# Router of a product-key expert layer: 136 of 256 candidate sums, and expert numbers by a sum and a smallest absolute value

## Chip, cores and metric

One core of a Trainium2 chip runs the whole kernel, in one launch. The metric is the device time of that launch in microseconds (us).

## What is computed

A two-layer diffusion backbone works on 512 latent tokens and 256 context tokens, each a row of 1024 values. In each layer three token mixers (differential attention, a two-way mLSTM, a short gated convolution) are merged, and then comes an expert layer with product keys. The change lies in the router of that expert layer. Cut to what matters, with N tokens, 8 heads and K = 16:

```python
q = (x @ wq).reshape(N, 8, 2, 128)
s = einsum('nhpd,hpkd->nhpk', q, keys)               # 2 x 128 scores for a token and head
top_s, top_i = lax.top_k(s, K)                       # the 16 best of each half, sorted
cand = top_s[:, :, 0, :, None] + top_s[:, :, 1, None, :]
best_s, best = lax.top_k(cand.reshape(N, 8, K * K), K)
i1 = take_along_axis(top_i[:, :, 0], best // K, -1)
i2 = take_along_axis(top_i[:, :, 1], best % K, -1)
expert = i1 * 128 + i2                               # 16 experts for a token and head
gate = softmax(best_s)
# then, for each token t and each of its 8 * 16 experts e:
# y[t] += gate * gelu(u_tab[e] . x[t]) * v_tab[e]
```

The tables `u_tab` and `v_tab` have 16384 rows of 1024 values in each layer. The context's output isn't needed in layer 1, so the experts run for ten tiles of 128 tokens: six in layer 0 and four in layer 1.

## The kernel before

**Tiles and stages.** Tokens lie on the 128 partitions, in tiles of 128. Two tiles are a pair: pair 0 is the context, pairs 1 and 2 are the latents. A stage is a generator in the program of each engine (`norm1`, `qkv`, `da`, `mlp`, `ml`, `mc`, `mln`, `merge`, `route`), for one layer and one or more pairs. `schedule()` (L117) writes the order of stages out by hand, in segments. At the end of nearly every stage stands a barrier across TensorE, VectorE and ScalarE (L1496 on VectorE), which SyncE waits for too.

**Expert groups between the steps.** The expert work of a routed tile is cut into 64 groups of two experts per token (`GS = 2`). A group is: two indirect transfers of GpSimd (L1131), each of which gathers one row of 8 KB for each of 128 tokens (1 MB) into a ring of 8 slots; two dot products on VectorE (L2055); gelu, weights and two small diagonal matrices on ScalarE (L1471 to L1478); eight TensorE products (L796) that add the rows up and free the two slots. `walk()` (L347) puts groups between the steps of stages: after step n of a stage come as many groups as the table `QUOTAS` says, and this table is computed when the kernel is built, from estimated step costs (`steps()`, L83) that the change doesn't touch. So each engine has one fixed order of work. ScalarE and TensorE treat a group one place later than VectorE (`LAG_ACT` and `LAG_PE`).

**The five routing stages.** `route` runs five times, each time for one pair, with 8 heads of 4 steps: layer 0 for pairs 0, 1 and 2, layer 1 for pairs 1 and 2. The quotas give them 0, 25, 48, 41 and 29 groups. In this text they are called route A to route E, in this order. In the fourth, the groups come in bursts: 8 after head 1, 7 after head 2, 5 and 6 later, and then one or two after each step. GpSimd may gather for head h of a tile only when VectorE has written that head's expert numbers (semaphore `routed`, L2028).

**What a head costs, by engine.** TensorE makes queries and scores (L758 and the chains of L436), ScalarE copies them out (L1413, L1420) and takes the exponentials (L1425). VectorE does the rest, in `route` (L1968), for both tiles of the pair:
- steps 1 and 2: `top16` (L1953) on each half of the scores. For each tile it takes the maximum of 8, finds their places, replaces them, takes 8 more and finds their places: five passes over 128 scores, ten for two tiles;
- step 3: the 64 places found become floats (L2005), the 16 x 16 sums are made for two tiles in one instruction of 512 elements (L2006), `top16` makes its ten passes over 256 sums each, and a shift (L2011) and a mask (L2012) split a place into its two coordinates;
- step 4: the coordinates become floats (L2015), and each is turned into a key number by comparing with 0 to 15 (L2018), multiplying (L2021) and adding up (L2024), each of these as two instructions of 512 elements; then times 128 plus the layer's base (L2026), and the sum (L2028). `gates` of the head before follows (L1989, L1991).

Between these passes stand `drain` instructions, so that each reads what the one before has written.

Of the kernel before, what the change touches and what calls it, by code (L numbers as in the profile page):

```python
# [8 lines left out]
D, SEQ, CTX, DEPTH, P = 1024, 512, 256, 2, 128  # L9
# [10 lines left out]
PH, NK, TOPK, PEER_N = 8, 128, 16, 16384  # L20
ADA_W = 384
BIG = 1e30
RS = 8
GS = 2
GROUPS = PH * TOPK // GS
# [175 lines left out]
def build(nc, io):  # L201
    fp32, u32 = mybir.dt.float32, mybir.dt.uint32
    ALU, ACT, AX = mybir.AluOpType, mybir.ActivationFunctionType, mybir.AxisListType
    es = ExitStack()
    with es:
        sbuf = es.enter_context(nc.sbuf_tensor("arena", [P, 53200], fp32))
# [5 lines left out]
        def sem(name):  # L212
            return es.enter_context(nc.semaphore(name))
# [3 lines left out]
        def s(name):  # L217
            if name not in S:
                S[name] = sem(name)
            return S[name]  # L220

        def view(base, shape, parts=P):
            n = int(np.prod(shape))
            ap = sbuf[0:parts, base:base + n]
            if len(shape) == 2:
                return ap.rearrange("p (a b) -> p a b", a=shape[0])
            if len(shape) == 3:
                return ap.rearrange("p (a b c) -> p a b c", a=shape[0], b=shape[1])
            return ap
# [6 lines left out]
        def keep(n):  # L236
            at[0] += n
            return at[0] - n
# [14 lines left out]
        LAM = view(keep(DEPTH), [DEPTH])  # L253
        SS, MS, RT = view(keep(24), [24]), view(keep(24), [24]), view(keep(24), [24])
        MX, NM, SUM, RC, RL, INV0 = (view(keep(2), [2]) for _ in range(6))
        IOTA = view(keep(TOPK), [TOPK])
        N1A = view(keep(DEPTH * 2 * KD), [DEPTH, 2, KD])
        N1B = view(keep(DEPTH * 2 * KD), [DEPTH, 2, KD])
        N1G = view(keep(DEPTH * KD), [DEPTH, KD])
# [16 lines left out]
        IDX = sbuf[:, keep(NT * P):at[0]].bitcast(u32).rearrange("p (a b) -> p a b", a=NT)  # L276
# [5 lines left out]
        DN = at[0]  # L282
        RING_AT = 53200 - RS * 2 * D
        RING = view(RING_AT, [RS, 2 * D])
        DENSE = RING_AT - DN
# [57 lines left out]
        w_in = [sem(f"w_in{i}") for i in range(WSLOTS)]  # L343
        gathered = [sem(f"gathered{i}") for i in range(RS)]
        ROT = range(2, 8)
# [460 lines left out]
        def _(sp):  # L806
# [13 lines left out]
            def const(dst, src):  # L820
                sp.dma_start(dst, src).then_inc(s("const_in"), 16)
                n_const[0] += 16
# [7 lines left out]
            const(CVCW.rearrange("p a b c -> p (a b c)"), io["cvcw"])  # L830
            const(GATEB, io["gate_b"])
            const(N1G.rearrange("p a b -> p (a b)"), io["n1g_cols"])
            const(IOTA, io["iota"].to_broadcast([P, TOPK]))
            assert n_const[0] == CONST_DMAS * 16

            def ada_rows_by_group(l, g):
# [2 lines left out]
            for q in range(AQ):  # L839
                if q >= 2:  # L840
                    sp.wait_ge(s("ada_mm"), q - 1)
                for g in range(4):
                    i = (q % 2) * 4 + g
# [264 lines left out]
        def _(pool):  # L1108
# [7 lines left out]
            pool.affine_select(out=MASK[:, 0, :], in_=MASK[:, 0, :], compare_op=ALU.is_ge, fill=BIG, base=0, pattern=[[1, P]], channel_multiplier=-1)  # L1116
            pool.affine_select(out=MASK[:, 1, :], in_=MASK[:, 1, :], compare_op=ALU.is_ge, fill=BIG, base=0, pattern=[[-1, P]], channel_multiplier=1)
            for half in range(2):
# [365 lines left out]
        def _(dve):  # L1484
            V_ = nc.vector
            TT, TSC, STT = V_.tensor_tensor, V_.tensor_scalar, V_.scalar_tensor_tensor
# [6 lines left out]
            def bc(ap, shape):  # L1493
                return ap.to_broadcast(shape)
# [458 lines left out]
            def top16(vals, idx, sco, work):  # L1953
                for v, i_, sc, w_ in zip(vals, idx, sco, work):
                    V_.max(v[:, 0:8], sc)  # L1955
                dve.drain()
                for v, i_, sc, w_ in zip(vals, idx, sco, work):
                    V_.max_index(i_[:, 0:8], v[:, 0:8], sc)  # L1958
                    V_.match_replace(w_, v[:, 0:8], sc, -3e38)  # L1959
                dve.drain()  # L1960
                for v, i_, sc, w_ in zip(vals, idx, sco, work):
                    V_.max(v[:, 8:16], w_)
                dve.drain()
                for v, i_, sc, w_ in zip(vals, idx, sco, work):
                    V_.max_index(i_[:, 8:16], v[:, 8:16], w_)  # L1965
                dve.drain()

            def route(kind, l, pairs):  # L1968
                (p,) = pairs
                t0 = 2 * p  # L1970
                area = buf(l, p, "RA", [8, PW])
                sco, scw = area[:, 4:6], area[:, 6:8]
                small = DN + PLACE[l, p]["RSM"]
                bs2, eb, nmx, ssum = view(small, [2, 2, TOPK]), view(small + 64, [2, 2, TOPK]), view(small + 128, [2, 2]), view(small + 132, [2, 2])
                small += 136
                tsh, tif = view(small, [2, 2, TOPK]), view(small + 64, [2, 2, TOPK])
                ixu = sbuf[:, small + 128:small + 192].bitcast(u32).rearrange("p (a b c) -> p a b c", a=2, b=2)
                bb = sbuf[:, small + 192:small + 288].bitcast(u32).rearrange("p (c a b) -> p c a b", c=3, a=2)
                bf, ie = view(small + 288, [2, 2, TOPK]), view(small + 352, [2, 2, TOPK])
                wide = DN + PLACE[l, p]["RW"]  # L1980
                cand, candw = (view(wide + 512 * i, [2, TOPK, TOPK]) for i in range(2))
                hot = (cand, candw)
                four = [P, 2, TOPK, TOPK]
                dve.wait_ge(s("h2_out"), nxt("h2_out", 32))
                dve.wait_ge(s("x1_out"), nxt("x1_out", 32))

                def gates(h):
                    dve.wait_ge(s("best_exp"), nxt("best_exp"))
                    V_.reciprocal(ssum[:, h % 2], ssum[:, h % 2])  # L1989
                    dve.drain()  # L1990
                    TT(GATE[:, t0:t0 + 2, h * TOPK:(h + 1) * TOPK], eb[:, h % 2], bc(ssum[:, h % 2].unsqueeze(2), [P, 2, TOPK]), ALU.mult)  # L1991
                    dve.drain().then_inc(s("gated"), 1)

                for h in range(PH):
                    bs_ = bs2[:, h % 2]
                    for pp in range(2):
                        n = 2 * h + pp
                        (b,), _, (f_,) = UNIT["s", l, p, n]
                        dve.wait_ge(bank_out[b], f_ + 1)
                        halves = [slice(i * P, (i + 1) * P) for i in range(2)]  # L2000
                        top16([tsh[:, pp, i, :] for i in range(2)], [ixu[:, pp, i, :] for i in range(2)],
                              [sco[:, pp, o] for o in halves], [scw[:, pp, o] for o in halves])
                        dve.drain().then_inc(s("top"), 1)
                        yield
                    V_.tensor_copy(tif, ixu)  # L2005
                    TT(cand, bc(tsh[:, 0].unsqueeze(3), four), bc(tsh[:, 1].unsqueeze(2), four), ALU.add)  # L2006
                    dve.drain()
                    flat = lambda a, i: a[:, i].rearrange("p a b -> p (a b)")
                    top16([bs_[:, i, :] for i in range(2)], [bb[:, 0, i, :] for i in range(2)], [flat(cand, i) for i in range(2)], [flat(candw, i) for i in range(2)])
                    TSC(nmx[:, h % 2].unsqueeze(2), bs_[:, :, 0:1], -1.0, None, ALU.mult)  # L2010
                    TSC(bb[:, 1], bb[:, 0], 4, None, ALU.logical_shift_right)  # L2011
                    TSC(bb[:, 2], bb[:, 0], 15, None, ALU.bitwise_and)  # L2012
                    dve.drain().then_inc(s("best"), 1)
                    yield
                    V_.tensor_copy(bf, bb[:, 1:3])  # L2015
                    dve.drain()
                    for i, o in enumerate(hot):
                        TT(o, bc(bf[:, i].unsqueeze(3), four), bc(IOTA.unsqueeze(1).unsqueeze(1), four), ALU.is_equal)  # L2018
                    dve.drain()
                    for i, o in enumerate(hot):  # L2020
                        TT(o, o, bc(tif[:, i].unsqueeze(2), four), ALU.mult)  # L2021
                    dve.drain()
                    for i, o in enumerate(hot):
                        V_.reduce_sum(ie[:, i], o, AX.X)  # L2024
                    dve.drain()
                    TSC(ie[:, 0], ie[:, 0], float(NK), float(l * PEER_N), ALU.mult, ALU.add)  # L2026
                    dve.drain()
                    TT(IDX[:, t0:t0 + 2, h * TOPK:(h + 1) * TOPK], ie[:, 0], ie[:, 1], ALU.add).then_inc(s("routed"), 1)  # L2028
                    if h:
                        gates(h - 1)  # L2030
                    if h == PH - 1:
                        gates(h)
                    yield
                barrier()
# [51 lines left out]
    return np.cos(ang).astype(np.float32), np.sin(ang).astype(np.float32)  # L2086


# [43 lines left out]
```

## Time and profile before

| | us |
|---|---|
| median of three runs | 5707.03 |
| lowest and highest of them | 5704.67, 5711.7 |
| span of the profiled execution | 5713.0 |

The profile page gives no other time for the profiled execution than its span, so the span stands for it: 6.0 us above the median of the runs and 1.3 us above the highest. TensorE is busy for 72% of the span, VectorE for 51%, ScalarE for 30% and GpSimd for 25%. No engine is busy all the time, because the stages have different limits. The chain that ended last is made of TensorE's chains of products (L436, 25% of the span), the gathers (18%), TensorE's products for the groups (L796, 9%) and VectorE's dot products (L2055, 6%), and then of many small shares, VectorE's top-16 lines among them. How to read such a profile here: the share of an engine over the whole span says little; the question is what binds in each of the five routing stages, and so most of the rows below are cut to those stretches.

### The profile page before, as it was taken

Reading aid. Unit: us, or ns where it says so; the run is one execution under the profiler, and the core shown is the slowest. Engines: PE = TensorE matmul, PEld = TensorE weight load, DVE = VectorE, ACT = ScalarE, POOL = GpSimd, SP = SyncE. Lnnn points to the kernel's source line nnn. Section 1 sums busy time; section 2 is a strip of 40 time slices with the busy share of each in tenths; the row PEclk is TensorE's granted clock in tenths of the full one; section 3 lists DMA queues with packets and bytes.
Section 4 is the critical chain, followed back from the end, with each engine's and each line's share of the span. In section 5 each row is a group of like instructions: output and inputs, shape, how many; then the busy total and the mean of one; then the engine's idle time right before and its main releaser. Section 6 shows DMA issues by size and latency. Waiting matters only on the chain.

```text
span 5713.0 us, 63933 instructions
## 1 busy us (share of the span) xinstructions
PE 4133.3 (72%) x22248; PEld 2503.9 (44%) x22248; DVE 2896.5 (51%) x6835; ACT 1716.0 (30%) x4747; POOL 1446.2 (25%) x1295
## 2 busy tenths in 40 slices
PE   3889668889896687658566677778566797645555
PEld 1678545566573354324222234667324564311111
DVE  1321757635447745874455443321685445954454
ACT  0200126333343343333322222200234253322222
POOL 0000012212222233333344341000231222345443
PEclk7879879979998898879788788759778898877777
DMA  6425448747798799999999995114896799899998
GB/s 256 160 107 173 158 167 295 269 170 295 288 370 326 287 409 395 390 364 383 371 416 411 396 421 221 48 41 162 316 370 236 282 401 372 307 359 421 403 421 353
DMA packets 259316, 1712.66 MB, mean 300 GB/s; under 512 B 37712, under 2 KB 39344, under 8 KB 71600
## 3 DMA queue, kind: packets, MB, share of 16 engines
q0 software_dynamic: 184320, 1342.26, 59.0%
q1 hardware_dynamic: 74672, 366.31, 17.4%
q8 instruction: 176, 2.88, 0.2%
q14 instruction: 148, 1.21, 0.1%
HBM read 1690.43 MB, written 17.92 MB: 299 GB/s over the span
## 4 chain that ended last, share of the span: by engine, by line
PE 41%; DMA 22%; DVE 17%; ACT 6%; issue 4%; DVEq 4%; POOL 3%; ACTq 2%; PEld 1%; SPq 1%; PEldq 0%; POOLq 0%
PE psum L436 25%; DMA arena<-in_uv,arena 18%; PE psum L796 9%; DVE arena L2055 6%; POOL arena L1131 3%; DMA arena<-in_w_ada 1%; DVE arena L1965 1%; DVE arena L1958 1%; PEld psum L436 1%; PE psum L396 1%; DVE arena L1959 1%; PE psum L617 1%; PE psum L618 1%; ACT arena L1226 1%; DMA arena<-in_w_mix 1%
## 5 line engine op out<-in xcount | busy, mean ns | idle before, releaser
L1131 POOL DMA_INDIRECT arena<-in_uv,arena x1280 | 1442.3, 1127 | 4231.1 <-PE psum L796 2795.7
L796 PE MATMUL psum<-arena 64*64 64x512 f32 x10240 | 1559.2, 738 | 934.0 <-ACTq L1478 854.4
L2055 DVE CUSTOM_DVE_ANT_0 arena<-arena 128x1024 f32<-128x1024 f32 x1280 | 1547.2, 1226 | 1121.4 <-DMA arena<-in_uv,arena 1055.0
L436 PE MATMUL psum<-arena 128*128 128x256 f32 (+2 forms) x8480 | 1958.0, 389 | 111.1 <-DVEq L1497 80.9
L436 PEld LDWEIGHTS psum<-arena 128*128 128x128 f32 (+1 forms) x8480 | 1618.6, 195 | 563.6 <-issue 192.0
L796 PEld LDWEIGHTS psum<-arena 64*64 64x64 f32 x10240 | 388.1, 156 | 1864.1 <-ACTq L1478 1176.1
L1471 ACT ACTIVATE arena<-arena 128x2 f32<-128x2 f32 x640 | 130.8, 204 | 1620.4 <-DVEq L2057 1605.0
L1477 ACT ACTIVATE arena<-arena 128x64 f32<-128x64 f32 x1280 | 375.9, 340 | 46.1 <-issue 2.1
L396 PE MATMUL psum<-arena 128*128 128x128 f32 (+1 forms) x680 | 128.1, 343 | 298.4 <-DVE arena L1556 102.5
L1474 ACT ACTIVATE arena<-arena 128x1 f32<-128x1 f32 x1280 | 307.9, 287 | 45.1 <-issue 0.7
L1917 DVE TENSOR_TENSOR arena<-arena,psum 128x256 f32<-128x256 f32 x120 | 50.6, 421 | 460.3 <-ACT arena L1381 458.6
L396 PEld LDWEIGHTS psum<-arena 128*128 128x128 f32 (+1 forms) x680 | 96.6, 177 | 353.2 <-issue 154.3
L1471 ACT ACT_TABLE_LOAD x158 | 202.7, 1283 | 31.9 <-DVEq L2057 28.2
L1381 ACT ACTIVATE arena<-psum 128x256 f32<-128x256 f32 x120 | 46.0, 384 | 394.8 <-PE psum L436 394.6
L2055 DVE DVE_READ_ACCUMULATOR2_ANT arena<- 128x1 f32 x1280 | 105.8, 83 | 0.0
L1381 ACT ACT_TABLE_LOAD x69 | 88.5, 1283 | 51.5 <-PE psum L436 42.5
L1955 DVE MAX8 arena<-arena 128x8 f32<-128x128 f32 (+1 forms) x240 | 69.6, 332 | 67.8 <-ACT arena L1420 55.4
L1612 DVE TENSOR_REDUCE arena<-psum 128x2 f32<-128x1536 f32 (+1 forms) x40 | 61.8, 1545 | 73.9 <-PE psum L522 73.4
L1205 ACT ACTIVATE arena<-psum 128x256 f32<-128x256 f32 x68 | 26.1, 384 | 226.0 <-PE psum L436 225.9
L537 PE MATMUL psum<-arena 128*128 128x128 f32 x416 | 66.2, 314 | 35.9 <-ACT arena L1235 35.9
L1170 ACT ACTIVATE arena<-arena 128x1024 f32<-128x1024 f32 x22 | 23.2, 1057 | 213.1 <-DMA arena<-in_ctx 90.3
L758 PEld LDWEIGHTS psum<-arena 128*128 128x128 f32 x320 | 47.7, 210 | 87.3 <-issue 48.1
(210 smaller groups left out, 2765.2 us busy)
## 6 DMA issues: line engine op xcount, KB each, us to landing
arena<-in_w_in SPq DMA_DIRECT2D x92, 1024.0 KB, 6.1
arena<-in_w_mix SPq DMA_DIRECT2D x120, 768.0 KB, 6.5
arena<-in_w_ada SPq DMA_DIRECT2D x32, 1536.0 KB, 16.3
arena<-in_w_wq SPq DMA_DIRECT2D x40, 1152.0 KB, 8.6
arena<-in_w_wo SPq DMA_DIRECT2D x20, 1024.0 KB, 8.1
arena<-in_uv,arena POOLq DMA_INDIRECT x1280, 10.7
arena<-ada_rows SPq DMA_DIRECT2D x15, 512.0 KB, 5.8
arena<-x_rows SPq DMA_DIRECT2D x14, 512.0 KB, 6.0
```

The source lines that it names most:

```text
L396: return mm(out, in_, IDENT[0:n, 0:n], start=True, stop=True, is_transpose=True)
L436: ins = mm(out, a, b, start=(i == 0), stop=(i == last))
L537: ins = mm(psum[:, 3840:3840 + P], wt[:, kt * P:(kt + 1) * P], V[:, kt, h * P:(h + 1) * P], start=(kt == 0), stop=(kt == nk - 1))
L796: ins = mm(psum[o, r_ * 512:r_ * 512 + 512], DIAG[rows, c, :], RING[rows, sl, D + half * 512:D + (half + 1) * 512], start=first, stop=last ...
L1131: pool.indirect_dma_start(RING[:, sl, :], None, io["uv"], bass.IndirectOffsetOnAxis(IDX[:, t, h * TOPK + k:h * TOPK + k + 1], 0)).then_inc ...
L1381: A.activation(sig[:, n % 4, :], bank(b, PW), ACT.Sigmoid).then_inc(s("sig"), 1)
L1471: A.activation(GELU[:, c0:c0 + GS], ACTS[:, c0:c0 + GS], ACT.Gelu)
L1474: A.activation(WGT[:, c:c + 1], GELU[:, c:c + 1], ACT.Copy, scale=GATE[:, t, h * TOPK + k:h * TOPK + k + 1])
L1477: A.activation(DIAG[:, c, :], PAIR, ACT.Copy, scale=WGT[:, c:c + 1])
L1612: V_.reduce_max(MX, psum[:, 1024:3072].rearrange("p (m n) -> p m n", m=2)[:, :, 0:nk], AX.X)
L1955: V_.max(v[:, 0:8], sc)
L2055: V_.tensor_tensor_reduce(out=RING[:, sl, 0:D], in0=RING[:, sl, 0:D], in1=XT[:, u % 2, :], scale=1.0, scalar=0.0, op0=ALU.mult, op1=ALU.ad ...
```

## The change

The expert numbers stay the same. The 16 best of the 256 sums of two sorted lists of 16 lie among those pairs (i, j) with (i + 1)(j + 1) at most 16. The new kernel forms all pairs with j < 8 (128 sums, place 8 i + j) and the pairs (0, j) with j from 8 to 15 (8 sums, places 128 to 135), and looks for the best in these 136.

A place becomes two codes by a mask and a shift in one instruction each: the bits of i, scaled so that the code is 65536 i; and the bits of j, scaled so that the code is 65536 j, or 65536 (j + 120) for the last 8. From each list's key numbers the same codes are taken away beforehand, with a constant table `LOOKUP` that also holds the layer's base. Code plus table entry is then the key number where they belong together, and at least some 49000 in size elsewhere. So one instruction adds all 4 x 16 x 16 combinations, and one reduction takes the smallest absolute value of each 16. The last sum also multiplies by 128.

```diff
+CANDS, STEP = TOPK // 2, 65536
+NCAND = TOPK * CANDS + TOPK - CANDS
...
-        IOTA = view(keep(TOPK), [TOPK])
+        LOOKUP = view(keep(DEPTH * 2 * TOPK), [DEPTH, 2, TOPK])
...
-            const(IOTA, io["iota"].to_broadcast([P, TOPK]))
+            const(LOOKUP.rearrange("p l s k -> p (l s k)"), io["lookup"].to_broadcast([P, DEPTH * 2 * TOPK]))
...
-                bf, ie = view(small + 288, [2, 2, TOPK]), view(small + 352, [2, 2, TOPK])
+                codes, ie = view(small + 288, [4, TOPK]), view(small + 352, [2, 2, TOPK])
+                tables = view(small + 64, [4, TOPK])
                 wide = DN + PLACE[l, p]["RW"]
-                cand, candw = (view(wide + 512 * i, [2, TOPK, TOPK]) for i in range(2))
-                hot = (cand, candw)
-                four = [P, 2, TOPK, TOPK]
+                cand, candw = (view(wide + 2 * NCAND * i, [2, NCAND]) for i in range(2))
+                apart = view(wide, [4, TOPK, TOPK])
+                four = [P, 4, TOPK, TOPK]
...
-                    V_.tensor_copy(tif, ixu)
-                    TT(cand, bc(tsh[:, 0].unsqueeze(3), four), bc(tsh[:, 1].unsqueeze(2), four), ALU.add)
+                    TT(tif, ixu, bc(LOOKUP[:, l].unsqueeze(2), [P, 2, 2, TOPK]), ALU.subtract)
+                    near = [P, 2, TOPK, CANDS]
+                    TT(cand[:, :, 0:TOPK * CANDS].rearrange("p t (i j) -> p t i j", i=TOPK), bc(tsh[:, 0].unsqueeze(3), near), bc(tsh[:, 1, :, 0:CANDS].unsqueeze(2), near), ALU.add)
+                    TT(cand[:, :, TOPK * CANDS:NCAND], bc(tsh[:, 0, :, 0:1], [P, 2, TOPK - CANDS]), tsh[:, 1, :, CANDS:TOPK], ALU.add)
                     dve.drain()
-                    flat = lambda a, i: a[:, i].rearrange("p a b -> p (a b)")
-                    top16([bs_[:, i, :] for i in range(2)], [bb[:, 0, i, :] for i in range(2)], [flat(cand, i) for i in range(2)], [flat(candw, i) for i in range(2)])
+                    top16([bs_[:, i, :] for i in range(2)], [bb[:, 0, i, :] for i in range(2)], [cand[:, i, :] for i in range(2)], [candw[:, i, :] for i in range(2)])
                     TSC(nmx[:, h % 2].unsqueeze(2), bs_[:, :, 0:1], -1.0, None, ALU.mult)
-                    TSC(bb[:, 1], bb[:, 0], 4, None, ALU.logical_shift_right)
-                    TSC(bb[:, 2], bb[:, 0], 15, None, ALU.bitwise_and)
+                    TSC(bb[:, 1], bb[:, 0], (TOPK - 1) * CANDS, 13, ALU.bitwise_and, ALU.logical_shift_left)
+                    TSC(bb[:, 2], bb[:, 0], TOPK * CANDS + CANDS - 1, 16, ALU.bitwise_and, ALU.logical_shift_left)
                     dve.drain().then_inc(s("best"), 1)
                     yield
-                    V_.tensor_copy(bf, bb[:, 1:3])
+                    V_.tensor_copy(codes, sbuf[:, small + 224:small + 288].bitcast(u32).rearrange("p (a b) -> p a b", a=4))
                     dve.drain()
-                    for i, o in enumerate(hot):
-                        TT(o, bc(bf[:, i].unsqueeze(3), four), bc(IOTA.unsqueeze(1).unsqueeze(1), four), ALU.is_equal)
+                    TT(apart, bc(codes.unsqueeze(3), four), bc(tables.unsqueeze(2), four), ALU.add)
                     dve.drain()
-                    for i, o in enumerate(hot):
-                        TT(o, o, bc(tif[:, i].unsqueeze(2), four), ALU.mult)
+                    V_.tensor_reduce(ie.rearrange("p a b c -> p (a b) c"), apart, AX.X, ALU.min, apply_absolute_value=True)
                     dve.drain()
-                    for i, o in enumerate(hot):
-                        V_.reduce_sum(ie[:, i], o, AX.X)
-                    dve.drain()
-                    TSC(ie[:, 0], ie[:, 0], float(NK), float(l * PEER_N), ALU.mult, ALU.add)
-                    dve.drain()
-                    TT(IDX[:, t0:t0 + 2, h * TOPK:(h + 1) * TOPK], ie[:, 0], ie[:, 1], ALU.add).then_inc(s("routed"), 1)
+                    STT(IDX[:, t0:t0 + 2, h * TOPK:(h + 1) * TOPK], ie[:, 0], float(NK), ie[:, 1], ALU.mult, ALU.add).then_inc(s("routed"), 1)
...
+def lookup_codes():
+    code = np.arange(TOPK)
+    far = np.where(code < CANDS, code, code + TOPK * CANDS - CANDS)
+    rows = [(code * STEP, far * STEP - l * PEER_N) for l in range(DEPTH)]
+    return np.array(rows, dtype=np.float32).reshape(1, -1)
```

## Rows read from the trace of the kernel before

**Rows 1.** Busy time by stretch: routes A to E, then part of the last stretch.

```profile
core 0: us, PE busy (x) PEld busy (x) DVE busy (x) ACT busy (x) POOL busy (x), PEclk, DMA share, GB/s
625.80:746.50 120.70, 51.13 (x200) 41.72 (x198) 107.70 (x447) 12.83 (x50) 7.84 (x8) 0.72 0.30 117
1762.00:1942.00 180.00, 105.03 (x568) 56.05 (x564) 162.90 (x541) 57.04 (x170) 41.85 (x43) 0.82 0.77 295
2264.00:2540.00 276.00, 189.10 (x1070) 84.97 (x1068) 237.79 (x701) 97.04 (x314) 103.43 (x96) 0.82 0.98 394
4006.00:4293.00 287.00, 167.36 (x937) 82.27 (x935) 219.52 (x669) 89.22 (x280) 90.88 (x86) 0.80 0.88 347
4810.00:5019.00 209.00, 140.02 (x747) 69.80 (x745) 189.08 (x618) 73.84 (x222) 65.02 (x58) 0.81 0.86 329
5100.00:5660.00 560.00, 309.57 (x1760) 72.37 (x1752) 275.65 (x446) 147.15 (x558) 275.43 (x219) 0.76 1.01 416
```

**Rows 2.** Timeline of VectorE, one head of route A: start us, us, what.

```profile
684.06 0.20 DVE L2005 CAST arena<-arena 128x64 f32<-128x64 uint32 x1 [0.17 <-issue]
684.17 0.69 DVE L2006 TENSOR_TENSOR arena<-arena 128x512 f32<-128x512 f32 x1
684.93 0.76 DVE L1955 MAX8 arena<-arena 128x8 f32<-128x256 f32 x2
...
690.08 1.29 DVE L2018 TENSOR_TENSOR arena<-arena 128x512 f32<-128x512 f32 x2
691.45 1.29 DVE L2021 TENSOR_TENSOR arena<-arena 128x512 f32<-128x512 f32 x2
...
694.44 0.19 DVE L2028 TENSOR_TENSOR arena<-arena 128x32 uint32<-128x32 f32 x1
694.54 0.16 DVE L1989 RECIPROCAL arena<-arena 128x2 f32<-128x2 f32 x1
```

**Rows 3.** Expert numbers (L2028), first and last start: routes A, B and E.

```profile
L2028 DVE TENSOR_TENSOR arena<-arena x8: 192/193/194, 625.8 to 746.5; 128x32 uint32<-128x32 f32 x8
...
L2028 DVE TENSOR_TENSOR arena<-arena x8: 192/192/195, 1770.2 to 1942.3; 128x32 uint32<-128x32 f32 x8
...
L2028 DVE TENSOR_TENSOR arena<-arena x8: 192/193/194, 4831.8 to 5019.3; 128x32 uint32<-128x32 f32 x8
```

**Rows 4.** VectorE's waits for gathers in route C, then D: us, times, longest.

```profile
DVE arena L2055 <- DMA arena<-in_uv,arena: 11.4, 10, 2.9
...
DVE arena L2055 <- DMA arena<-in_uv,arena: 41.6, 23, 6.1
```

**Rows 5.** Page, issues of gathers: count, median us from issue to landing.

```profile
arena<-in_uv,arena POOLq DMA_INDIRECT x1280, 10.7
```

**Rows 6.** VectorE's groups of instructions over the span, by line and shape.

```profile
L1955 DVE MAX8 arena<-arena 128x8 f32<-128x128 f32 x160 | 39.3, 287 | 64.7 <-ACT arena L1420 55.4 <-issue 2.5
L1955 DVE MAX8 arena<-arena 128x8 f32<-128x256 f32 x80 | 30.3, 420 | 3.1
L2006 DVE TENSOR_TENSOR arena<-arena 128x512 f32<-128x512 f32 x40 | 27.4, 685 | 0.0
L2067 DVE TENSOR_TENSOR arena<-arena 128x1024 f32<-128x1024 f32 x10 | 12.3, 1227 | 1.0
L2024 DVE TENSOR_REDUCE arena<-arena 128x32 f32<-128x512 f32 x80 | 51.2, 682 | 2.9
L1592 DVE TENSOR_REDUCE arena<-arena 128x8 f32<-128x1024 f32 x10 | 12.2, 1220 | 0.8
```

**Rows 7.** Three pieces of route D, columns as in rows 1.

```profile
4006.00:4030.00 24.00, 22.11 (x109) 19.10 (x107) 15.76 (x66) 5.82 (x15) 0.31 (x1) 0.99 0.37 136
...
4042.00:4060.00 18.00, 7.93 (x52) 2.85 (x56) 13.63 (x26) 6.37 (x21) 3.31 (x3) 0.57 0.67 260
...
4124.00:4160.00 36.00, 19.97 (x108) 10.21 (x112) 28.89 (x87) 12.04 (x39) 7.91 (x9) 0.76 0.83 347
```

More of the change, by code:

```diff
@@ L2122 @@
     arrays["gate_b"] = lay(a["ml_gate_b"].reshape(DEPTH, 16).T)
-    arrays["iota"] = np.arange(TOPK, dtype=np.float32).reshape(1, TOPK)
+    arrays["lookup"] = lookup_codes()
     arrays["uv"] = np.concatenate([a["peer_u"], a["peer_v"]], axis=-1).reshape(DEPTH * PEER_N, 2 * D)
```

## Prediction, made before the changed kernel was run

> **What bounds the kernel now.** The change touches VectorE's work in the five routing stages alone, so I asked of each of them whether VectorE is what it waits for. First I read the busy times by stretch [rows 1]. In route A, without expert groups, VectorE is busy for 107.7 of 120.7 us, 89%. The timeline of one head there shows what the other 11% are: gaps of some 0.08 us between instructions that depend on each other, and no wait for another engine [rows 2]. So about 90% is what a VectorE that is never kept waiting looks like in this code. The eight heads follow each other at (746.5 - 625.8) / 7 = 17.2 us [rows 3], while TensorE is busy for 42% and the DMA engines for 30% [rows 1]. Route A is VectorE's alone.
>
> Routes B and E read in the same way: VectorE is busy for 162.9 of 180 us and for 189.1 of 209 us, 90% in both [rows 1], with heads every 24.6 and 26.8 us [rows 3]. The DMA engines are at 0.77 and 0.86. In both VectorE binds too, with the gathers close behind in E.
>
> Routes C and D differ. In C the DMA share is 0.98 and VectorE is at 86%; it waits ten times for a gather, 11.4 us in all. In D, with its bursts of groups, the share is 0.88 and VectorE is at 76%, with 41.6 us of waits for gathers [rows 1, 4]. Both are bound mainly by the gathers.
>
> What can hide or take back a gain is thus the gathers. A transfer lands 10.7 us after its issue in the median [rows 5]. The ring holds four groups; in E 29 groups take 209 us, so a slot comes round after about 4 x 7.2 = 29 us, and there is time to spare as long as the DMA engines themselves aren't full.
>
> **The change part by part, for one head.** Durations are those of the profiled execution.
>
> - Top 16 of 136 sums in place of 256. A pass over 128 elements takes 287 ns and one over 256 takes 420 [rows 6], 1.04 ns per element. The other two kinds of pass differ by as much. Ten passes are each shorter by 120 elements: 10 x 120 x 1.04 = 1.25 us less.
> - The sums. From the cast to the first maximum pass 684.93 - 684.06 = 0.87 us go by [rows 2]. The new order is a subtraction of 64 elements in place of the cast, a sum of 256 and one of 16. An instruction that the next one doesn't depend on costs its elements and little more: the second of two of 512 elements adds 1.29 - 0.69 = 0.60 us [rows 2], 0.07 beyond 512 x 1.04. So 0.13 + 0.33, then 0.17 for the last with 0.08 for the gap behind it: 0.71 us, 0.16 less.
> - Place to expert number. From the first comparison to the instruction behind the expert number go by 694.54 - 690.08 = 4.46 us [rows 2]. That was six instructions of 512 elements and two small ones with five gaps. The new order is an addition of 1024 elements (1.23 us, as L2067), a reduction of 1024 (1.22, as L1592 [rows 6]), two gaps and a last instruction that holds the engine for 0.10: 2.71 us, 1.75 less.
> - At no cost: the masks with shifts in place of mask and shift alone (both two small instructions), the cast of 64 elements before and after, and the constant table, 192 bytes more per partition in one of ten loads at the start, which lie beside the first loads of weights. If that cover were gone, it would be below 1 us, once.
>
> Together 1.25 + 0.16 + 1.75 = 3.2 us per head, and 40 heads have 127 us less of VectorE's time.
>
> The prices that no row shows are the reduction with absolute value and minimum, and the addition with both inputs repeated by their patterns. The sum of 512 at L2006 repeats both inputs in the same way and takes 685 ns, no more per element than L2067, which repeats none [rows 6]. I take the plain prices: every row of rows 6 lies at 1.04 ns per element whatever the operation. For the range the reduction may cost double (1.2 us more per head), and the drains that fall away may give 0.2 us more: 2.0 to 3.4 us per head. By the Trainium skill ("Vector Engine (DVE) Microarchitecture Reference", section "Measured stream behaviour on trn2") a source runs at full rate only if its elements come in adjacent pairs, and at about 1.7 ns per element otherwise; if that held for a repeated element, it would take 0.9 us per head from the gain. L2006 speaks against it.
>
> **By stage.** Nothing is moved between engines or queues, no wait is added, and the order of groups stays.
>
> - A: 8 x 3.17 = 25.4 us. Behind VectorE nothing is near: TensorE would be at half the time.
> - B: 25.4 us less of VectorE's work. The DMA engines need 0.77 x 180 = 139 us, 0.90 of the remaining 155: free to follow. I take 25.
> - C: the DMA engines stand idle for 0.02 x 276 = 5.5 us. I take 3; the rest of the 25 turns into waits for gathers.
> - D: idle are 0.12 x 287 = 34 us, but not all behind the router. 15 lie before the first gather [rows 7], where one head of VectorE is in the way: 3.2. Another 6 us lie at 4042 to 4060, where VectorE waits for the first gathers: nothing. At 4124 to 4160 it is 6.1 us behind one head's work: 3.2, and about as much in the smaller gaps. I take 9.
> - E: the DMA engines need 0.86 x 209 = 180 us, 0.98 of the 184 that would be left, as in C. I take 22 of the 25.4.
>
> In the two stages with a busy DMA, E and C, a group's transfer is late next. The sum is 25.4 + 25 + 3 + 9 + 22 = 84 us. Against the profiled execution (5713.0 us span) that is 5629; the median of the runs is 6 us lower, and I predict from it: 5707 - 84 = 5623 us.
>
> **Rivals.**
>
> 1. *The gathers cap the mixed stages earlier.* If mixed traffic of gathers and weights didn't get past the 347 GB/s of D, then E needs 329 x 209 / 347 = 198 us and gains 11, C nothing, D 3.2, A and B 25 each: 64 us, 5643. For it speaks that no stretch around routes A, B, D, E ran faster; against it the 394 of C, which has weights as well, and the 416 of the last stretch [rows 1]. Chance 0.12. The Trainium skill ("DMA: Bandwidth & Descriptors", section "Where 436 GB/s comes from") puts the limit for loads from HBM at about 358 GB/s for a core, which would leave E 17 us and give 5637; the trace's 416 disagrees.
> 2. *The new additions run at half rate* because of the repeated elements: 1280 x 1.04 = 1.3 us more, 1.8 left per head. A, B, E give 15 each, C 3, D 6: 54 us, 5653. L2006 is against it. Chance 0.06. By the Trainium skill's rule on adjacent pairs ("Vector Engine (DVE) Microarchitecture Reference", "Measured stream behaviour on trn2") it would be 5644; again L2006 disagrees.
> 3. *What is gained in B and E is given back* in the stretches that follow, since those are full of gathers (the 1.01 [rows 1]). Then A and the first head of D stay: 28.6 us, 5678. Against it: the transfers of the following stretch can't be issued before the stage's last groups, so its start moves with the stage. Chance 0.05.
> 4. *Slower: the reduction with absolute value or the wide addition is not streamed at one element per step.* The gain is used up when both take 3.17 us more for their 2048 elements, 2.6 ns per element instead of 1.04. At 4.2 ns, four steps, a head gains -3.2 us; 24 heads of A, B, E lose 77, C and D about 20: 5804. No row has such an operation, but the plain forms of both run at 1.04. Chance 0.03.
> 5. *The change doesn't do what it says*, so that the passes aren't shorter or something else of the same size comes in: 5707. Chance 0.02.
>
> **How the numbers follow.** The likeliest case has 0.72, and its own range is 5605 (all of 25.4 in A, B and E, 5.5 in C, 14 in D, and 3.4 per head instead of 3.2) to 5650 (a reduction at double price: 16 each in A, B, E, 3 and 6). Rival 1 lies inside. Taking in most of rival 2 gives 5602 to 5655; left out are rivals 3 to 5 and some of the likeliest case, under 0.2. A measurement of this kernel can tell about 0.2%, 11 us, from no change. Faster by more than that: 0.72 + 0.12 + 0.06 + 0.05 = 0.95. Within: 0.02. Slower: 0.03.
>
> **What would show it.** VectorE's busy time falls by about 125 us; its passes over 136 sums take about 296 ns, the addition and the reduction of 1024 about 1.22 us each. Route A's heads follow at 14.1 us, B's at 21.4, E's at 23.6 to 24.2. In C the heads keep their distance and the waits of L2055 for gathers grow by some 20 us; in E they appear for the first time. The DMA share of B is 0.90, of E 0.97. I am wrong if a 1024 instruction takes over 2 us, if route E's heads stay above 25 us, or if routes C and D together give over 25 us.

## The result, and the profile after

The changed kernel takes 5616.23 us in the median (5613.76 to 5620.99, four runs) against 5709.36 us of the kernel before beside it: ratio 0.983, 95% interval 0.9813 to 0.9846, 93 us less. The forecast was 5623 us and 84 us less. Two later comparisons on other occasions gave ratios of 0.9832 (0.9812 to 0.9852) and 0.9828 (0.9809 to 0.9847). In these the kernel before took 5719.96 and 5719.12 us and the gain was 103 to 104 us; it is the kernel before that differs from one occasion to the next, while the changed one stays at 5616.

First the prices. VectorE's groups of instructions over the span, by line and shape (columns as in rows 6):

```profile
L2021 DVE TENSOR_TENSOR arena<-arena 128x1024 f32<-128x1024 f32 x40 | 49.1, 1226 | 3.5 <-issue 0.4
L2023 DVE TENSOR_REDUCE arena<-arena 128x64 f32<-128x1024 f32 x40 | 48.8, 1221 | 3.5 <-issue 0.4
L1957 DVE MAX8 arena<-arena 128x8 f32<-128x136 f32 x80 | 20.4, 296 | 3.2
L1960 DVE FIND_INDEX8 arena<-arena 128x8 uint32<-128x136 f32 x80 | 23.6, 294 | 0.0
```

The wide addition takes 1226 ns and the reduction with absolute value and minimum 1221 ns: what the plain instructions of 1024 elements cost before [rows 6]. A pass over 136 sums takes 296 ns. The timeline of VectorE in route A, one head (start us, us, what; answers to rows 2):

```profile
675.87 1.23 DVE L2021 TENSOR_TENSOR arena<-arena 128x1024 f32<-128x1024 f32 x1
677.17 1.22 DVE L2023 TENSOR_REDUCE arena<-arena 128x64 f32<-128x1024 f32 x1
678.47 0.19 DVE L2025 SCALAR_TENSOR_TENSOR arena<-arena 128x32 uint32<-128x32 f32 x1
678.58 0.16 DVE L1992 RECIPROCAL arena<-arena 128x2 f32<-128x2 f32 x1
...
685.59 0.23 DVE L2008 TENSOR_TENSOR arena<-arena 128x64 f32<-128x64 uint32 x1 [0.17 <-issue]
685.74 0.42 DVE L2010 TENSOR_TENSOR arena<-arena 128x256 f32<-128x256 f32 x1
686.07 0.17 DVE L2011 TENSOR_TENSOR arena<-arena 128x16 f32<-128x16 f32 x1
686.31 0.51 DVE L1957 MAX8 arena<-arena 128x8 f32<-128x136 f32 x2
```

From the addition to the instruction behind the expert number it is 678.58 - 675.87 = 2.71 us (forecast 2.71), and the sums take 686.31 - 685.59 = 0.72 us (forecast 0.71).

VectorE is busy for 2777.6 us of the whole execution, 118.9 less than before (2896.5).

Then where the time went. The instruction that writes the expert numbers marks the heads, as in rows 3; here are the routes A to E of the changed kernel, eight heads each, first and last start:

```profile
L2025 DVE SCALAR_TENSOR_TENSOR arena<-arena x8: 192/194/194, 620.7 to 720.9; 128x32 uint32<-128x32 f32 x8
...
L2025 DVE SCALAR_TENSOR_TENSOR arena<-arena x8: 192/193/194, 1741.2 to 1891.9; 128x32 uint32<-128x32 f32 x8
...
L2025 DVE SCALAR_TENSOR_TENSOR arena<-arena x8: 193/194/228, 2247.0 to 2481.1; 128x32 uint32<-128x32 f32 x8
...
L2025 DVE SCALAR_TENSOR_TENSOR arena<-arena x8: 192/193/194, 3976.2 to 4219.4; 128x32 uint32<-128x32 f32 x8
...
L2025 DVE SCALAR_TENSOR_TENSOR arena<-arena x8: 192/194/194, 4753.5 to 4919.4; 128x32 uint32<-128x32 f32 x8
```

And the same instruction of the kernel before in C and D, which rows 3 left out:

```profile
L2028 DVE TENSOR_TENSOR arena<-arena x8: 192/193/194, 2297.1 to 2537.4; 128x32 uint32<-128x32 f32 x8
...
L2028 DVE TENSOR_TENSOR arena<-arena x8: 192/194/194, 4029.2 to 4292.8; 128x32 uint32<-128x32 f32 x8
```

The lead of the changed kernel over the one before is the difference of two such times: 25.6 us at A's last head, 50.4 at B's last, 50.1 at C's first, 56.2 at C's last, 53.0 at D's first, 73.4 at D's last, 78.3 at E's first and 99.9 at E's last. The spans of the two executions differ by 5713.0 - 5613.6 = 99.4. The head that comes before the first mark of a route shows in the step between two routes. So A and B give what was forecast, C gives 6 us that are gone again before D's first head (although that head's own work is 3 us shorter), D gives about 20 us within its marks, and E gives 22 within them; 5 come between D's last head and E's first, of which that head's own work is 3.

The busy times between these marks, routes A to E (columns as in rows 1):

```profile
620.80:721.00 100.20, 51.70 (x216) 43.01 (x214) 86.65 (x419) 13.87 (x55) 7.66 (x8) 0.78 0.36 141
1741.20:1891.90 150.70, 100.19 (x552) 55.26 (x544) 134.60 (x497) 55.38 (x164) 45.72 (x40) 0.86 0.88 337
2247.00:2481.20 234.20, 160.16 (x912) 70.38 (x912) 188.16 (x585) 87.48 (x278) 93.80 (x84) 0.83 1.00 407
3976.20:4219.40 243.20, 144.55 (x839) 62.81 (x837) 183.24 (x579) 84.27 (x270) 97.83 (x86) 0.80 0.97 389
4753.60:4919.40 165.80, 118.95 (x652) 59.18 (x644) 148.88 (x523) 68.37 (x202) 59.09 (x52) 0.84 0.93 362
```

VectorE is still busy for 89% in B and 90% in E. Here is the line that comes first among VectorE's waits in C, in D and in E (columns as in rows 4):

```profile
DVE arena L2052 <- DMA arena<-in_uv,arena: 29.0, 25, 2.9
...
DVE arena L2052 <- DMA arena<-in_uv,arena: 42.6, 24, 5.1
...
DVE arena L2052 <- issue: 5.4, 27, 0.7
```

In C the waits for gathers grew from 11.4 us to 29.0: that is where most of C's share of the saved work went. In E there are none, where I had expected the first. In D they stayed where they were (41.6, now 42.6), though VectorE is busy for 183 us between its marks instead of 204. That was not in the forecast, and most of the experiments are about it. D between its marks in the kernel before, to compare with the fourth row above:

```profile
4029.20:4292.80 263.60, 145.25 (x828) 63.17 (x828) 204.26 (x607) 83.40 (x265) 90.88 (x86) 0.78 0.93 365
```

Two corrections to the section on the kernel before. ScalarE treats a group one place later than VectorE, but TensorE two places later (`LAG_ACT, LAG_PE, LAG_TAIL = 1, 2, 3`). And the bursts in D are of 8, 7 and 5 groups, each after a whole head; there is no burst of 6.

### The profile page after: what moved, and what is told of

It reads as the page before. It is cut to its first block, busy times and chain, and to the rows that moved or that the text cites. A ratio compares the mean times of both kernels' runs of the same rounds, so it can differ in the third digit from the quotient of the medians.

```text
span 5613.6 us, 63693 instructions
## 1 busy us (share of the span) xinstructions
PE 4129.5 (74%) x22248; PEld 2501.0 (45%) x22248; DVE 2777.6 (49%) x6675; ACT 1716.9 (31%) x4747; POOL 1473.9 (26%) x1295
## 3 DMA queue, kind: packets, MB, share of 16 engines
q1 hardware_dynamic: 74672, 366.33, 17.6%
## 4 chain that ended last, share of the span: by engine, by line
PE 42%; DMA 23%; DVE 16%; ACT 6%; issue 4%; POOL 2%; DVEq 2%; ACTq 2%; PEld 2%; SPq 1%; PEldq 0%; POOLq 0%
PE psum L438 26%; DMA arena<-in_uv,arena 19%; PE psum L798 10%; DVE arena L2052 6%; POOL arena L1133 2%; DMA arena<-in_w_ada 1%; PEld psum L438 1%; PE psum L398 1%; DVE arena L1967 1%; DVE arena L1960 1%; DVE arena L1961 1%; DMA arena<-in_norm_g 1%; PE psum L619 1%; PE psum L620 1%; ACT arena L1228 1%
## 5 line engine op out<-in xcount | busy, mean ns | idle before, releaser
L1133 POOL DMA_INDIRECT arena<-in_uv,arena x1280 | 1470.0, 1148 | 4104.1 <-PE psum L798 2675.5
L2052 DVE CUSTOM_DVE_ANT_0 arena<-arena 128x1024 f32<-128x1024 f32 x1280 | 1548.3, 1226 | 1140.5 <-DMA arena<-in_uv,arena 1068.4
L524 PE MATMUL psum<-arena 64*128 64x256 f32 (+1 forms) x288 | 66.7, 581 | 26.0 <-ACT arena L1228 23.1
```

What stands on the lines that cost most here:

```text
L524: ins = mm(psum[:, 1024 + m * 1024 + a:1024 + m * 1024 + b], qt[rows, h, i * P:(i + 1) * P], KT[rows, h, a:b], start=True, stop=True)
L1133: pool.indirect_dma_start(RING[:, sl, :], None, io["uv"], bass.IndirectOffsetOnAxis(IDX[:, t, h * TOPK + k:h * TOPK + k + 1], 0)).then_inc ...
L2052: V_.tensor_tensor_reduce(out=RING[:, sl, 0:D], in0=RING[:, sl, 0:D], in1=XT[:, u % 2, :], scale=1.0, scalar=0.0, op0=ALU.mult, op1=ALU.ad ...
```

## Experiments

**One routing stage back to the old code.** Four kernels, each the changed one, with the old steps 3 and 4 in some stages (and the old table `IOTA` beside `LOOKUP`, one small load more at the start):

```diff
+OLD_ROUTES = ((1, 1),)      # D; ((0, 0), (0, 1)) is A and B, ((0, 2),) C, ((1, 2),) E
...
+                    if (l, p) in OLD_ROUTES:
+                        V_.tensor_copy(tif, ixu)
...
+                    else:
                         TT(tif, ixu, bc(LOOKUP[:, l].unsqueeze(2), [P, 2, 2, TOPK]), ALU.subtract)
```

Routes A and B old:

> The new kernel with the old steps 3 and 4 in routes A and B alone. If the two routes are bound by VectorE alone and nothing is given back behind them, this costs 2 x 25.4 us against the new kernel: 5616 + 51 = 5667 us, heads of A every 17.2 us and of B every 24.6. If part of B's gain is given back in the stretch full of gathers behind it, the cost is smaller: about 46 (5662), which is what remains of the difference between the two traces of before and after when route C begins.

Route C old:

> The new kernel with the old steps 3 and 4 in route C alone. Theory (C is bound by the gathers, and a gain there is only queued transfers that are used up before route D): 0 to 3 us slower than the new kernel, 5616 to 5619. Rival (VectorE sets C's pace in part, as the 6 us between its first and last expert number say): 6 us or more, 5622.

Route D old:

> The new kernel with the old steps 3 and 4 in route D alone. Theory (in D the routing work of each head and the burst of groups behind it are in series, since the slots come free only after VectorE's dot products, so each us of VectorE's work counts): 24 us slower than the new kernel, 5640, and every interval between heads grows by about 3 us. Rival (my forecast: most idle time of the DMA engines there doesn't hang on VectorE): 9 us, 5625, and the first interval with a burst stays at 49 us.

Route E old:

> The new kernel with the old steps 3 and 4 in route E alone. Theory (VectorE binds, the DMA share of 0.94 in the new kernel leaves room): 25.4 us slower, 5641, no waits for gathers in either. Rival (forecast: gathers take over for part of it): 22 us, 5638, with waits of several us for gathers in the new kernel.

The changed kernel did not run beside these four. It ran twice more beside other kernels, with medians of 5616.12 and 5616.30 us; "cost" is the difference to 5616.2. The four runs of each kernel lie up to 15 us apart, so a cost is good to some us and no better. The span is the time from the first to the last mark of the stages put back.

| old in | median us | cost | forecast term | span of the stage, new | span, old |
|---|---|---|---|---|---|
| A and B | 5660.92 | 45 | 50.4 | 98.5 and 150.6 | 120.6 and 172.0 |
| C | 5617.64 | 1 | 3 | 233 to 237 | 240.0 |
| D | 5641.71 | 25 | 9 | 243 to 246 | 262.3 |
| E | 5643.17 | 27 | 22 | 165.7 | 188.0 |

The costs add up to 98 us, against 5717.6 - 5616.2 = 101 for the whole change beside these runs. The first interval of A is 13.8 us in most executions, so that A's span is 98.5; the profiled one had 15.5 there.

For A and B the spans differ by 22.1 + 21.4 us within the marks, and by one head before each, which makes 50; the median gives 45. The runs of that kernel lie between 5651.90 and 5667.19 us and so hold both values that were expected: whether some us are given back behind B isn't shown. C is nearly free, as forecast. E costs all of VectorE's work. D costs 25 by the median and 16 to 19 by its span, with 3 more for the head before its first mark; its first interval with a burst grew from 49 to 53.2 us, and even the fastest of its runs (5630.82) lies above the 5625 of my forecast, which fell.

**Why D.** The forecast had put the DMA engines' pause after the first gathers (a pause is a time in which they stand nearly idle) down to VectorE waiting for them. Here is VectorE when it comes to that burst, before and after, with the first gather into a freed slot on GpSimd. Kernel before:

```profile
4045.94 0.19 DVE L2028 TENSOR_TENSOR arena<-arena 128x32 uint32<-128x32 f32 x1
...
4046.70 1.23 DVE L2055 CUSTOM_DVE_ANT_0 arena<-arena 128x1024 f32<-128x1024 f32 x1 [0.23 <-issue]
...
4056.06 1.44 POOL L1131 DMA_INDIRECT arena<-in_uv,arena  x1 [16.38 <-PE psum L796]
```

Changed kernel:

```profile
3990.07 0.19 DVE L2025 SCALAR_TENSOR_TENSOR arena<-arena 128x32 uint32<-128x32 f32 x1
...
3990.83 1.23 DVE L2052 CUSTOM_DVE_ANT_0 arena<-arena 128x1024 f32<-128x1024 f32 x1 [0.23 <-issue]
...
4000.19 0.94 POOL L1133 DMA_INDIRECT arena<-in_uv,arena  x1 [13.79 <-PE psum L798]
```

VectorE doesn't wait: the first slots have landed while it routed the head, and it starts on them at once. Its waits come later in the burst, when it has used up the landed slots and takes the new ones as they land; the longest, in the kernel before, is here:

```profile
4062.78 1.25 DVE L2055 CUSTOM_DVE_ANT_0 arena<-arena 128x1024 f32<-128x1024 f32 x1 [6.08 <-DMA arena<-in_uv,arena]
```

The next gather goes out 10.1 us after that head's expert numbers in both kernels (4056.06 - 4045.94, 4000.19 - 3990.07). So the gathers wait for VectorE here, not the other way round, and the 3 us by which the head became shorter come off the pause. Two pauses of the DMA engines in D, before (columns as in rows 1, DMA share last but one):

```profile
4052.00:4059.00 7.00, 6.93 (x40) 2.44 (x44) 4.54 (x8) 3.81 (x15) 2.38 (x2) 0.61 0.16 33
4153.00:4162.00 9.00, 6.98 (x44) 2.26 (x48) 7.56 (x14) 4.65 (x19) 2.61 (x2) 0.62 0.18 45
```

and the same two in the changed kernel:

```profile
3999.00:4002.00 3.00, 3.00 (x27) 1.05 (x24) 1.91 (x4) 0.69 (x3) 1.51 (x2) 0.74 0.25 63
4095.00:4100.00 5.00, 5.00 (x45) 1.31 (x37) 3.89 (x8) 2.54 (x11) 2.82 (x2) 0.88 0.21 48
```

They shrank from some 7 and 9 us to 3 and 5 (to whole us). Two theories of what holds the slots were open: the lag of the other engines, or the burst itself.

**The lag.** The edit is `LAG_ACT, LAG_PE, LAG_TAIL = 0, 1, 3`.

> The changed kernel with ScalarE's part of a group right behind VectorE's and TensorE's one place later (before: one and two places). Theory for route D: after a burst the last two groups hold four of the eight slots while VectorE routes the next head, so that the gathers run dry; with one group held, the three intervals with bursts get 3 to 5 us shorter each, and D's span falls from 243 to some 232 us. Rival (the gathers themselves fill D's time by now): D's span stays at 240 or above. In A nothing changes; in B, C and E ScalarE may wait for VectorE's dot products before it copies scores, which would cost 1 to 2 us per group there, so the whole may well be slower.

Measured: 5750.15 us, ratio 1.0055 (1.0038 to 1.0071), so slower than the kernel before. D's span is 4342.4 - 4098.5 = 243.9 us, as in the run of the changed kernel beside it. The head in front of the first burst has its expert numbers at 4112.38, and this is the next gather:

```profile
4122.49 0.94 POOL L1133 DMA_INDIRECT arena<-in_uv,arena  x1 [13.79 <-PE psum L798]
```

That is 10.1 us behind them once more, so the theory that the lag holds the slots fell. What the shorter lag costs lies elsewhere: 1086 us go by between A's last head and B's first, against 1017 in the run of the changed kernel beside it, and 40, 19 and 12 us more between the later routes. In the first of these stretches ScalarE waits for VectorE's dot products 60 times, 271.6 us in all, against 15 times and 85.4 us. That it thereby serves the mixers late is how I read it; I didn't test it.

**The burst.** In D the bursts of 8, 7 and 5 are spread out, two groups after each step until as many have gone as in the old order, and none is moved to another stage:

```diff
                     want = max(done, min(want, routed_upto(items, st[1], st[2], max(0, (n + 1) // 4 - 1))))
+                    if (st[1], st[2]) in FIRST_ROUTES:
+                        want = max(done, min(want, 2 * (n - 6)))
```

On the changed kernel:

> The changed kernel with the groups of route D spread out: two after each step from head 1's last on, in place of bursts of 8 and 7 after a whole head; as many groups in each stage. Theory (a full ring of landed slots waits while VectorE routes a whole head, so the gathers pause, 2.6 and 4.5 us in the new kernel): the pauses go and D's span falls from 243.5 to 235 to 238 us, the whole by 5 to 8 us. Rival (the pauses are only moved, since two groups a step make VectorE wait for gathers before the next expert numbers are there): D's span stays within 2 us of 243.5.

On the kernel before:

> The kernel before with the same spreading. Its pauses were 6.1, 1.6, 7.7, 0.8 and 1.4 us. Theory: D's span falls from 263.6 by 12 to 18 us, to about 249, the whole to a ratio of 0.997 to 0.998. If so, D's gain by the change was the shortening of these pauses. Rival: VectorE's work counts in full in D however the groups lie, and D stays at 260 or above.

The changed kernel beside them:

> The changed kernel once more, as the point of comparison for the runs beside it: ratio 0.983 to the kernel before, span of route D 243 to 244 us.

| | median us | ratio to before, interval | D's span |
|---|---|---|---|
| before (13 runs) | 5719.12 | | 263.6 |
| before, spread | 5701.16 | 0.9973 (0.996 to 0.9985) | 240.9 |
| changed | 5616.30 | 0.9828 (0.9809 to 0.9847) | 244.7 |
| changed, spread | 5606.44 | 0.9817 (0.9797 to 0.9837) | 236.7 |

Busy times between the marks of D, first the kernel before spread, then the changed kernel spread (in bursts the DMA share is 0.93 before and 0.97 after):

```profile
4024.80:4265.80 241.00, 144.88 (x824) 62.73 (x824) 204.05 (x608) 83.29 (x265) 94.78 (x86) 0.81 0.99 399
```

```profile
3966.40:4203.10 236.70, 148.16 (x839) 62.80 (x837) 183.91 (x580) 84.20 (x270) 95.75 (x86) 0.83 1.00 400
```

The medians of the two changed kernels are 10 us apart with runs that just overlap; D's span tells them apart better. With VectorE's work untouched at 204 us the spread order alone takes 22.7 us from D, more than I expected (12 to 18), and the DMA share is 0.99. On top of it the change is worth 240.9 - 236.7 = 4 us in D instead of 20. These are spans of one execution each, and D's span is 243 to 246 us in all six executions that have the changed kernel's code and order in D. The medians of the whole say the same more weakly: the change is worth 5701.16 - 5606.44 = 95 us in the spread order, and 103 in bursts. So it was the order of routing and groups that made each us of VectorE's routing count in D: a whole head is routed while the ring fills and then lies idle, then the burst runs. Where the two alternate in small steps, the gathers set the pace and the saving turns into waits.

**The two halves of the change.** First the new step from place to number with all 256 sums (`CANDS = TOPK`, a shift by 12 in place of 13, no second sum); then the search in 136 sums, with compare and product as before, against a small table that has 128 to 135 for the last eight places.

> The new step from place to expert number with all 256 sums (half of the change). By my terms a head saves 1.75 us of 3.17: heads of A every 15.5 us, and 1.75 / 3.17 = 0.55 of the gain: 51 us of 93, ratio 0.991. Rival (the gain has a threshold, since the gathers take over after the first us in D and E): more than 60 us of the gain come with this half.

> The search in 136 sums, with places turned into expert numbers by compare and product as before (the other half of the change). A head saves 1.25 + 0.16 = 1.4 us: heads of A every 15.8 us; 0.45 of the gain, 42 us, ratio 0.9925. If halves add up, this and the other one give 93 us together; if the gathers cap the gain, they give more than that together.

The changed kernel beside them:

> The changed kernel once more, as the point of comparison on this chip: 0.983 of the kernel before, and route spans (first to last expert number) of 98.5, 150.6, 234, 243 and 165.7 us.

| | median us | ratio, interval | gain us | spans of A, B, C, D, E |
|---|---|---|---|---|
| before | 5719.96 | | | 120.7, 172.1, 240.3, 263.6, 187.5 |
| new numbers, 256 sums | 5661.23 | 0.990 (0.9884 to 0.9917) | 59 | 108.6, 159.5, 237.3, 252.5, 175.5 |
| 136 sums, old numbers | 5668.70 | 0.991 (0.9894 to 0.9927) | 51 | 111.8, 161.5, 236.1, 254.5, 177.4 |
| both | 5616.12 | 0.9832 (0.9812 to 0.9852) | 104 | 99.6, 150.6, 235.8, 243.9, 165.7 |

(Spans of "before" from its first profile.) In A the heads follow at 15.5 and 15.8 us, as worked out. Both gains are some 8 us above what I had said, as the whole gain is 104 us in this comparison and not 93. Their sum, 110 us, exceeds the whole by 6 us, which is within the intervals. In A, B, D and E the spans add up: in D 11.1 + 9.1 = 20.2 of 19.7. Only C shows a cap: each half alone brings the 3 to 4 us that both bring together.

**Step costs that fit the shorter stage.**

```diff
-        return [(7.0 if (l, pairs) in FIRST_ROUTES else 5.0)] * (4 * PH)
+        return [(6.0 if (l, pairs) in FIRST_ROUTES else 4.0)] * (4 * PH)
```

> The changed kernel with the routing steps entered at 4.0 and 6.0 in place of 5.0 and 7.0 in the table of step costs, since they have become shorter: routes B, C, D, E get 21, 41, 39 and 26 groups in place of 25, 48, 41 and 29, the stages around them the rest. What leaves E (3 groups of 2.4 us of VectorE's time) shortens it by 7 us, what leaves B by 10, and merge, which TensorE binds, gets longer by the TensorE time of these groups, about 1.2 us each (7 groups: 8 us). I expect 0 to 10 us less than the changed kernel; no change if TensorE's clock or the gathers take it back.

Measured: 5593.43 us (5585.73 to 5602.36), ratio 0.9794 (0.9774 to 0.9815), 23 us below the changed kernel beside it, whose runs lay between 5612.36 and 5618.99. It beats both kernels. The spans of B, C, D and E are 139.8, 210.7, 232.2 and 157.4 us, together 57 us less than in that changed kernel, and the stages between them take over half of it back: from B's last head to C's first it takes 378 us instead of 353, from D's last to E's first 551 instead of 538. I had put the price of such groups in merge too low (8 us for 7 of them) and the gain of the whole too low as well.

Why the stages from A's last head to B's first got 16 us shorter with more groups in them is open; in the executions of the other kernels with unchanged lags and quotas before B this stretch takes between 1012 and 1027 us. TensorE's granted clock was 0.92 of full speed in it, against 0.90 in the changed kernel beside it, and among the others the longest stretch has the lowest clock (0.89) and the shortest the highest (0.91); what sets that clock here I don't know. Nor did I give the kernel before the lower step costs, so that it isn't shown that they help because the routing steps became shorter.

## Why the prediction was right, and where it was not

- *A pass over 136 sums, the sums, the expert numbers: 3.17 us per head.* Right in each term (296 ns, 0.72 and 2.71 us), and A's heads follow at 14.1 us as forecast.
- *The reduction and the wide addition have no price in the trace; the plain prices are taken.* Right: 1221 and 1226 ns. Rivals 2 and 4 are out. The addition repeats both inputs by its patterns and takes as long as L2067, which repeats none (1227). So the rule of the Trainium skill on adjacent pairs ("Vector Engine (DVE) Microarchitecture Reference", section "Measured stream behaviour on trn2") doesn't reach elements that are read again at once; no run here tests it on elements that lie apart. The forecast read more out of its rows than they say: 1.04 ns per element is the step from a short instruction to a longer one ((1227 - 685) / 512 = 1.06 at the additions), and each has some 0.14 us on top, so that L2006 at 685 ns costs more per element than L2067.
- *A 25.4 and B 25.* The spans and leads bear this out (25.6, and 24.8 more by B's last head); by the median of the kernel with both put back it is 45 together, with runs that hold 50 as well. Rival 3 is out: of B's lead of 50.4 us 50.1 are left at C's first head, and of E's 99.9 the spans of the whole still show 99.4.
- *C 3, the rest turns into waits for gathers.* Right: 1 us by the median, and 17.6 us more of waits.
- *E 22, since the DMA share would reach 0.98.* A little low: it rose to 0.93, no wait for a gather appeared, and all 25 us count. Rival 1 is out: D ran at 389 GB/s and E at 362, where it had set a cap of 347. So is, for this core on its own, the limit of about 358 GB/s in the Trainium skill ("DMA: Bandwidth & Descriptors", section "Where 436 GB/s comes from"): C ran at 407.
- *D 9.* This is the step that failed. It said of the 6 us at 4042 to 4060: "where VectorE waits for the first gathers: nothing", and beside that it counted one head's 3 us before the first gather and some 6 us in the later gaps. The trace of before has VectorE start on landed slots without a wait at 4046.70; I had taken the 41.6 us of waits for the whole stage to lie there. Put back alone, D costs 25 us; the spread order shows why. Idle time of the DMA engines in D isn't a property of the gathers but of the order: the pauses are as long as VectorE keeps a full ring waiting. They explain some 11 of the 20 us, not all: between the marks the idle time fell from 0.07 x 263.6 = 18 to 0.03 x 243.2 = 7 us, but the DMA engines' share times the span fell from 0.93 x 263.6 = 245 to 0.97 x 243.2 = 236 us as well. A part of that is traffic that fell outside the marks (365 x 263.6 = 96.2 MB, 389 x 243.2 = 94.6 MB); the rest stays open.
- *What would show it.* VectorE's busy time fell by 119 us (forecast about 125), heads follow at 14.1, 21.5 and 23.7 us in A, B and E (14.1, 21.4 and 23.6 to 24.2), and the DMA share is 0.88 in B and 0.93 in E (0.90 and 0.97). One sign of being wrong was "if routes C and D together give over 25 us". By the leads they give 73.4 - 50.1 = 23 us, by the medians of the kernels put back 1 + 25 = 26: it stands at its edge, where the forecast had 12.

The sum of 84 us thus came out 9 us low in the comparison it was made against, with D 11 to 16 and E 3 to 5 us too low, C 2 and A with B up to 5 too high. Against the gains of 103 and 104 us on the other two occasions it is 20 low, at the edge of the stated range. That D's mistake stayed inside the range is in part luck: the range allowed 14 us for D, and the 20 to 25 that D gives fit in only because other terms (a full 25.4 in E, 3.4 us per head) had been given room for other reasons.

## What to carry to other kernels

A stage that another stream of work is woven into has no fixed answer to "what is a saved us worth": look at the order of the two. If they alternate in steps shorter than what the ring of buffers holds, the saving stops where the transfers are full (C, and D in the spread order); if a whole unit of work stands between two bursts, each us counts although the engine waits for transfers in the same stage (D in bursts). So a sum of waits over a stage must be placed in time before it is used to rule out a gain. And when a stage has become cheaper, it is worth trying to let the costs that a planner was given follow: here that brought 23 us more, though why isn't fully known, and spreading the bursts brought some 10.

## What was not expected of the hardware

In the changed kernel's first profile one instruction of route A (L2014) waited 1.5 us for nothing that the profile shows, and the first interval of A was 15.5 us. With the same code in A it was 15.5 in one more kernel's profile (the same instruction waited 1.5 us), 14.8 in one (it waited 0.9) and 13.8 in six. I have no experiment on it.
